# First attention layer: four modulation chunks computed as rows on TensorE, and the value product begun with the first four K-tiles

## What is computed

```python
c_act = jax.nn.silu(c)
mod = (c_act @ ada_w[layer] + ada_b[layer])[:, None, :]
sh_a, sc_a, gt_a, sh_m, sc_m, gt_m = jnp.split(mod, 6, axis=-1)
h = modulate(rms_norm(x, attn_norm[layer]), sh_a, sc_a)
mix = diff_attention(h, ...)      # (softmax(Q1 K1^T) - lambda softmax(Q2 K2^T)) V, 8 heads, RMSNorm, w_out
x = x + gt_a * mix
h = modulate(rms_norm(x, mlp_norm[layer]), sh_m, sc_m)
x = x + gt_m * squared_relu_mlp(h, mlp_w1[layer], mlp_w2[layer])
```

## Time and profile before

| | us |
|---|---|
| median of 3 runs | 1425.49 (1423.74 to 1425.61) |
| the profiled execution | 1421.12 |
| its span, first to last instruction | 1419.3 |
| granted TensorE clock, mean of the span | 0.968 of full |
| opening and first attention, up to the output projection | 156.0 |

### The profile page before, as it was taken

The page is one execution under the profiler, slowest core; times in us unless marked ns, Lnnn a source line. Parts: engine busy times, 40 slices in busy tenths (PEclk is TensorE's granted clock), DMA queues, the critical chain, the costliest instruction groups (busy, mean ns, idle before and its releaser), DMA issues. The chain is left out here.

```text
span 1419.3 us, 22085 instructions
## 1 busy us (share of the span) xinstructions
PE 1314.1 (93%) x8506; PEld 1136.6 (80%) x8506; DVE 876.9 (62%) x1546; ACT 678.7 (48%) x1184; POOL 170.4 (12%) x172
## 2 busy tenths in 40 slices
PE   6797989999989999899999878999999999899999
PEld 2687889888869865688998775699898777799987
DVE  2768678888675377696445674465555655555443
ACT  2354544334444356354544575464444565554442
POOL 0636101101000000010100121010000101011000
PEclk9889999999989899999999998999999999999999
DMA  9967639899866533259665251378655454376660
GB/s 351 317 211 248 199 104 331 291 326 321 288 194 175 172 117 93 81 159 301 178 194 158 87 184 34 103 193 261 188 171 185 135 178 133 92 206 184 188 178 30
DMA packets 249224, 267.42 MB, mean 188 GB/s; under 512 B 11040, under 2 KB 185376, under 8 KB 248736
## 3 DMA queue, kind: packets, MB, share of 16 engines
q1 hardware_dynamic: 246496, 263.52, 59.7%
q10 hardware_dynamic: 2624, 2.49, 0.5%
HBM read 264.83 MB, written 1.15 MB: 187 GB/s over the span
## 5 line engine op out<-in xcount | busy, mean ns | idle before, releaser
L1545 DVE TENSOR_TENSOR wlo<-wring,whi 128x1024 fp32r<-128x1024 f32 (+1 forms) x376 | 456.9, 1232 | 240.1 <-ACT whi L2607 239.4
L2607 ACT ACTIVATE whi<-wring 128x1024 fp32r<-128x1024 f32 (+1 forms) x376 | 388.8, 1043 | 360.4 <-PE ps_p L549 122.6
L547 PE MATMUL bank<-h_hi,whi 128*128 128x256 f32 x1216 | 351.5, 289 | 5.7 <-DVE h_lo L1699 2.3
L548 PE MATMUL bank<-h_lo,whi 128*128 128x256 f32 x1216 | 347.5, 286 | 0.0
L549 PE MATMUL bank<-h_hi,wlo 128*128 128x256 f32 x1216 | 347.1, 285 | 0.0
L547 PEld LDWEIGHTS bank<-h_hi,whi 128*128 128x128 f32 x1216 | 236.9, 195 | 11.8 <-issue 7.9
L548 PEld LDWEIGHTS bank<-h_lo,whi 128*128 128x128 f32 x1216 | 237.1, 195 | 0.7
L549 PEld LDWEIGHTS bank<-h_hi,wlo 128*128 128x128 f32 x1216 | 236.7, 195 | 0.0
L3244 POOL TENSOR_TENSOR ex<-ex 128x512 f32<-128x512 f32 x64 | 73.0, 1140 | 710.9 <-ACT g_hi L2716 710.9
L1767 DVE TENSOR_TENSOR g_lo<-ex,g_hi 128x512 fp32r<-128x512 f32 x64 | 45.0, 703 | 125.2 <-POOL ex L3244 125.0
L547 PE MATMUL bank<-whi,h_hi 128*128 128x512 f32 (+3 forms) x248 | 99.6, 402 | 14.4 <-DVE h_lo L1666 6.2
(11 more groups left out here) (375 smaller groups left out, 1878.8 us busy)
## 6 DMA issues: line engine op xcount, KB each, us to landing
wring<-in_mlp_w SPq DMA_DIRECT2D x128, 512.0 KB, 5.3
wring<-in_ada_w SPq DMA_DIRECT2D x96, 512.0 KB, 7.2
wring<-in_mlp_w_in SPq DMA_DIRECT2D x64, 512.0 KB, 4.8
wring<-in_mlp_w_out SPq DMA_DIRECT2D x64, 512.0 KB, 4.1
wring<-in_a_w_in SPq DMA_DIRECT2D x24, 512.0 KB, 5.7
wring<-in_moba_w_qkv SPq DMA_DIRECT2D x24, 512.0 KB, 4.4
wring<-in_kv_ada_w SPq DMA_DIRECT2D x16, 512.0 KB, 7.3
wring<-in_w_kv SPq DMA_DIRECT2D x12, 512.0 KB, 4.9
```

The costliest lines, as they stand in the source:

```text
L547: nc.tensor.matmul(out, lh, rh, start=first, stop=False)
L548: nc.tensor.matmul(out, lh, rl, start=False, stop=False)
L1545: v.tensor_tensor(piece_view(wlo, p), raw_view(p), piece_view(whi, p).bitcast(F32), ALU.subtract).then_inc(lo_ready, 1)
L2607: a.activation(piece_view(whi, p), raw_view(p), ACT.Copy).then_inc(hi_ready, 1)
```

## The change

1. No chunk is computed on POOL. DVE keeps chunks 4 (beside the value product) and 5 (in slot 4). Chunks 8, 9, 6 and 7 are computed as rows on PE, one each at the end of slots 0, 2, 5 and 7 (`ROW_SLOTS`, `ROW_CHUNKS`). Their columns are made at the end of the slot after (1, 3, 6, 8). ACT copies the row sums at the end of the row slot (into `xn`, which POOL used), DVE adds the bias two slots after it.
2. `weight_plan` puts all four loads of such a chunk behind the two loads of the head of that slot, where before the loads of two chunks were interleaved one each per head.
3. PE starts the value product's first two pieces (K-tiles 0 to 3) when the even halves are split, and waits for the odd halves ahead of the third piece. DVE writes `wlo` of piece t ahead of `split_odd` of tile t; ACT makes `whi` of piece 0 ahead of its first odd half. DVE goes up to two pieces further ahead during chunk 4.
4. `gate_rows("a0")` in slot 7 moves ahead of `diff_mix`. `late_rows` and `late_columns` of the second layer get numbers four higher. The number of loads and their bytes stay.

```diff
-MOD_SLOTS = (1, 4, 5)
+MOD_SLOTS = (1, 5)
+ROW_SLOTS = (0, 2, 5, 7)
+ROW_CHUNKS = (8, 9, 6, 7)
...
-             ada_part(4, 4), ada_part(8, 0), ada_part(4, 6)]
+             ada_part(4, 4), ada_part(4, 6)]
     for h in range(4):
-        plan += a_qk(h) + [ada_part(6, 2 * h), ada_part(*((8, 2 + 2 * h) if h < 3 else (9, 0)))]
+        plan += a_qk(h) + (ada(0, [ROW_CHUNKS[h // 2]]) if h % 2 == 0 else [])
     for j in range(4):
         plan += [a_v_part(1, j), ada_part(5, 2 * j)]
     for h in range(4, 8):
-        plan += a_qk(h) + [ada_part(7, 2 * h - 8)]
-        if h < 7:
-            plan += [ada_part(9, 2 * h - 6)]
+        plan += a_qk(h) + (ada(0, [ROW_CHUNKS[h // 2]]) if h % 2 == 0 else [])
...
-            turned("a0", TT - 1)
...
             for j in range(4):
+                if j % 2 == 0:
+                    pe.wait_ge(sem("a0_split"), TT + j)
                 token_piece(("a_v", 0), banks, h, j == 3)
...
+                if s == 7:
+                    gate_rows("a0", 16)
...
-                if s == 7:
-                    gate_rows("a0", 16)
-
-            pe.wait_ge(matvec_done, 4)
-            pool_columns([acc[:, 0, :]] + early[1], "early_mod", 2)
+                if s in ROW_SLOTS:
+                    late_rows(ROW_SLOTS.index(s))
+                if s - 1 in ROW_SLOTS:
+                    late_columns(ROW_SLOTS.index(s - 1))
+
...
             for t in range(TT):
+                keep_ahead("dve", t, 1)
                 split_odd("a0", t, outs)
-                keep_ahead("dve", t, 1)
...
             for j in range(4):
+                keep_ahead("dve", j, 3)
                 matvec(matvec_order[0], 2 * j, 2 * j + 2)
-                keep_ahead("dve", j)
...
-                    matvec(matvec_order[1 if head < 4 else 3], 2 * (head % 4), 2 * (head % 4) + 2)
                     keep_ahead("dve", p + 1)
...
+                if s - 2 in ROW_SLOTS:
+                    late_drain(ROW_SLOTS.index(s - 2))
...
-            pool_drain("early_mod", 7, 3, "ada_b0", 28)
+            late_drain(3)
...
+            keep_ahead("act", 0, 1)
             act.wait_ge(mod_drained, 4)
...
+                if s in ROW_SLOTS:
+                    late_sums(ROW_SLOTS.index(s))
```

More of the change, by code:

```diff
@@ L292, in build @@
                 "k": gate_row[:, :].rearrange("p (t c) -> p t c", t=TT)}
-        row_sums = [ex[:, :, :].rearrange("p a c -> p (a c)")[:, i * W:(i + 1) * W] for i in range(2)]
+        row_sums = [xn[:, i // 2, (i % 2) * W:(i % 2 + 1) * W] for i in range(4)]
+        row_sums += [ex[:, :, :].rearrange("p a c -> p (a c)")[:, i * W:(i + 1) * W] for i in range(2)]
         row_sums += [xn[:, 1, i * W:(i + 1) * W] for i in range(2)]
@@ L431, in build @@
         opening = (2, 3, 0, 1)
-        matvec_order = [ada_order[c] for c in (4, 6, 5, 7)] + ada_order[10:22] + ada_order[26:28]
-        drain_order = [ada_order[c] for c in opening + (4, 6, 5, 7, 8, 9)] + ada_order[10:]
+        matvec_order = [ada_order[c] for c in (4, 5)] + ada_order[10:22] + ada_order[26:28]
+        drain_order = [ada_order[c] for c in opening + (4, 8, 9, 5, 6, 7)] + ada_order[10:]
         def drained_by(*chunks):
             return max(drain_order.index(ada_order[c]) for c in chunks) + 1
-        early = (ada_order[8:10], [xn[:, 0, i * W:(i + 1) * W] for i in range(2)], xn[:, 1, 0:W])
-        late = ada_order[22:26]
+        late = [ada_order[c] for c in ROW_CHUNKS] + ada_order[22:26]
         ROOT_EIGHTH = math.sqrt(0.125)
@@ L463, in mod_columns @@
                                             start=True, stop=True)
[L464 to L473, removed]
                 last.then_inc(filled[b], 1)
@@ L1581, in mod_drain @@
                 v.memset(stat[:, 1:2], 0.0).then_inc(mod_drained, 1)
[L1583 to L1589, removed]
             def rstd(width, n, tag=None, eps=None):
@@ L2003, in diff_low, with late_drain @@
                                        ALU.mult, ALU.subtract).then_inc(sem("diff_low"), 1)
+            def late_drain(i):
+                key = ("late_mod", i)
+                layer, c = late[i]
+                src = bank_full(dve, key)
+                first, at = ada_index(late[i]), col["ada_b" + layer[3:]] + 4 * c
+                v.tensor_tensor(mod[:, 4 * first:4 * first + 4], src[:, 0:4], params[:, at:at + 4],
+                                ALU.add).then_inc(drained[uses[key][0]], 1)
+                bank_emptied(dve, key)
+                v.memset(stat[:, 1:2], 0.0).then_inc(mod_drained, 1)
             for j in range(4):
+                keep_ahead("dve", j, 3)
                 matvec(matvec_order[0], 2 * j, 2 * j + 2)
-                keep_ahead("dve", j)
             dve.wait_ge(sem("bias_in"), 16)
@@ L2774, in diff_high, with late_sums @@
                     sem("diff_high"), 1)
+            def late_sums(i):
+                key = ("late_rows", i)
+                a.activation(row_sums[i], bank_full(act, key), ACT.Copy).then_inc(drained[uses[key][0]], 1)
             for t in range(TT):
@@ L2812, in _ @@
             mlp("m0")
-            def late_sums(i):
-                key = ("late_rows", i)
-                a.activation(row_sums[i], bank_full(act, key), ACT.Copy).then_inc(drained[uses[key][0]], 1)
             norm("kv", [(h_hi, h_lo, gs, mod[:, 64:72]), (hk_hi, hk_lo, gs2, mod[:, 48:56])], 4, ready=(6, 8),
-                 last=last_of(("m0_w2", 7)), beside=late_sums)
+                 last=last_of(("m0_w2", 7)), beside=lambda t: late_sums(4 + t))
             def nsa_kv(w):
```

64 lines of the change are left out of this document (13 added, 51 removed).

## The result

The changed kernel takes 1439.16 us (1438.03 to 1441.93, four runs), the kernel before 1425.55 beside it: ratio 1.0097, 95% interval 1.0074 to 1.012, so 10.5 to 17.1 us slower. The forecast was 1432.9 with a range of 1424.0 to 1438.5: the direction was right, the size too small by 6.3 us, and the range ends 0.7 us too low.

A forecast was written before the change was run, and what follows sets the result against it. Bound by DMA rate until about 57 us, then by who gives back places in the ring of ten loads. Terms 0.85 + 1.75 + 4.45 + 0.4 - 1.85 + 1.8 = +7.4 us on 1425.49 gave 1432.9, range 1424 to 1438.5.

The forecast's parts named there:

- R(2): Eight row matmuls of chunk 6 on PE at the end of slot 5, booked at +1.75 us.
- low clock: PE's clock falls in slot 6's new wait and the work behind it runs slower: +1.8 us, bounds 0 and 3.1.
- Opening: Until about 57 us: value product ends 5.4 us early, all lost to later waits for transfers; booked at nothing.
- Rival 1: The early start survives and slot 6's two terms go: 1421.6 us, chance 0.17; decided if chunk 8's row matmuls end before 54.
- Price of a chunk: On PE's path, a chunk's row matmuls take 1.75 us (bounds 1.05 and 3.8), its columns one slot later 0.82.
- Slot 5: Head 5's first piece lands 2.3 us later, silent GpSimd gives 1.5 back; head 3's weights come at 121.75: +0.85 us.
- Slot 6: Main term: head 7's loads wait for R(2), so PE waits 3.8 us ahead of diff_back(3): +4.45 us.
- Slot 7: Its earlier 1.3 us of waiting goes and chunk 7's row matmuls come at its end: +0.4 us.
- GpSimd: Silent in slot 5, so DVE's next step and wlo return to their usual 1.53 and 1.22 us: 1.5 us back.
- Rival 3: Every block of row matmuls holds the stream; slot 6's stall returns in slots 1 and 3: +12, 1437.9 us, chance 0.13.
- Rival 2: Trade, no change: head 7's loads arrive just in time and the clock holds: +1.2, 1426.7 us, chance 0.14.
- sign of 2 us: Behind about 164 us the length stays as before; the forecast is wrong if it differs by over 2 us.

The follow-up runs named there:

- e3: Kernel before with only the early value product and its order of splits; chunks 8 and 9 stay on GpSimd: 1424.91 us, ratio 0.9998.
- e6: e2 with diff_combine of head 3 moved in DVE's slot 4 behind the second pair of chunk 5's steps: 1427.62 us.
- e12: e2 with loads of chunks 8, 9 behind heads 1, 3, their row matmuls ending slots 1, 2, and every late_drain right behind diff_even; second measurement: 1420.08 us.
- e1: Changed kernel with the drain of chunk 9's columns moved to the head of chunk 5's steps in DVE's slot 4: 1436.02 us.
- e9: Changed kernel with chunk 9's drain first, as in e1, and only chunk 6's four loads moved behind head 5's: 1424.82 us.
- e2: Changed kernel with chunk 9's drain first, as in e1, and loads of chunks 6 and 7 behind those of heads 5 and 7: 1422.17 us.
- e11_changed_again: Changed kernel as it is, measured again in five rounds beside the kernel before: 1439.84 us, ratio 1.0107.

## Why the prediction was wrong in size

By its own steps, forecast against the windows above and the earlier trace rows, in us; slot 5 is what the forecast's own dates give (110.0 to 130.05 against 16.9):

| step | forecast | measured |
|---|---|---|
| up to the start of slot 4 | +0.45 | +1.7 |
| slot 4 | -1.0 | -0.7 |
| slot 5 with R(2) | +3.15 | +8.6 |
| slot 6 with M | +4.45 | +5.6 |
| slot 7 with R(3) | +0.4 | +3.9 |
| slot 8 with M | -1.85 | -1.7 |
| low clock | +1.8 | in the slots |
| sum | +7.4 | +17.4 |

**Opening: right in what it books, in part by luck.** R(0) ends at 57.6 (57.4 forecast), head 1 starts at 60.55 (60.4), head 0's weights come at 78.95 (78.3). Nothing of the early start survives, and e3 shows it alone. But the value product starts at 36.2 (34.9 forecast) and ends at 49.5 (46.6): its first 5.1 us run at a granted clock of 0.52. And R(0) does not wait for its loads, as the forecast had it; PE reaches it late, at 55.7, and runs it in one go:

```profile
55.70 1.92 PE L701 MATMUL bank<-wring,pos_f 128*32 128x512 f32 x16
```

That its end is the forecast one is chance. That the transfers set the pace shows one step later, where head 1's product waits 2.9 us for `wlo` and ACT before it 6.7 us for the load. Rival 1 is out.

**Price of a chunk: right at the high clock.** R(2) takes 1.9 us (135.16 to 137.02; 1.75 forecast), M at the end of slot 3 0.9 (97.18 to 98.11; 0.82). At the low clock, in e6, a block takes 3.6 us, near the bound of 3.8. With four row blocks on PE e12 is faster than before.

**Slot 5: the step that failed,** "Weights at 121.75: +0.85". The turns came 9.3 us later than before, for two reasons. The first is a size: head 5's first piece came 5.2 us later (its `wlo` starts on DVE at 119.52, before at 114.29), not 2.3. I let the held loads of the block run in a row behind one release at 107, at 1.35 us each. The queue's timeline, then two windows of 1 us behind it:

```profile
108.08 2.01 SPq L3237 DMA_DIRECT2D wring<-in_ada_w  x3
```

```profile
113.00:114.00 1.00, 0.00 (x0) 0.00 (x0) 0.00 (x0) 0.00 (x0) 0.00 (x0) 1.00 0.80 262
...
115.00:116.00 1.00, 0.00 (x0) 0.00 (x0) 0.00 (x0) 0.00 (x0) 0.00 (x0) 1.00 1.13 353
```

The first of chunk 6's held loads goes out at 108.1, 1.1 us after the forecast's date, and from there to ACT's start on the piece it takes 10.3 us and not 8.4. The third load goes out 1.6 us behind the first (a later step of DVE releases it), and a load takes 1.5 to 2.0 us at 353 to 262 GB/s; which of the two makes the 1.9 us is not shown. Less the 1.5 us that the silent GpSimd gives, the piece makes the weights 3.7 us late (124.52). The second reason is a mechanism that the sum lacked and put at nothing: the product ahead of the wait takes a bank that the drain of chunk 9's columns gives back, and this drain stands on DVE behind the very work that PE would have waited for anyway. The kernel has PE wait for a drained bank whenever it takes one (`bank_take`); I had not asked where the drain stands in DVE's own queue. The wait and the product are then not side by side but in a row: 5.6 us more to the turns. e1 gives 5.3 of them back at the turns and 2.9 at the end of the slot, the rest goes to the low clock.

**Slot 6: right, and the main term for the forecast.** 3.8 us of wait forecast, 3.5 measured, for the reason given. e9 sharpens it: not the hold but the two loads ahead of head 7's piece made it long. M behind the wait runs at the low clock (148.10 to 149.66, 1.6 us for the 0.82 of the forecast).

**Slot 7: half missed.** Behind slot 6's wait the clock is low: the first product of slot 7 takes 4.8 us (149.66 to 154.45), its second 3.0 (155.73 to 158.69). The difference is the +1.8 of the sum. With `diff_back` and M of slot 6 at the low clock too (2.0 us for the forecast's 1.0) the low clock cost 2.8 us, inside its bounds of 0 and 3.1 but more than booked. A second wait for a drain (L895, 1.2 us) was not in it. With both, slot 7 comes to +3.4 of the +3.9. In e12, with the drains at the head, that wait is gone.

**GpSimd: right.** Its work in these slots is down to a few short steps for the heads' norms. Durations of `wlo` on DVE, min, median and max in ns from 30 to 200, against the earlier trace rows:

```profile
L1540 DVE TENSOR_TENSOR wlo<-wring,whi x34: 1214/1225/1227, 34.5 to 196.6; 128x1024 fp32r<-128x1024 f32 x34
```

It now never takes over 1.23 us in this stage; before, its longest was 2.32. The Trainium skill ("SBUF — State Buffer", section "SBUF: two separate sides") says that these two engines share ports; by it the longest `wlo` should fall to the usual one when GpSimd is silent, and it did: from 2.32 to 1.23 us. The gain was eaten: DVE was waiting for loads.

**The rivals.** Rival 3, that every R holds the stream, was priced at +12 and put into slots 1 and 3. The sum is nearer to its number than to mine, but not through its mechanism. R(1) does hold the stream, for 17.6 of SyncE's 50.9 us for L701 (in slot 2), and no stall of PE follows in slot 3 (9.27 busy of 9.31). R(2) holds it for 12.5, which is the wait of slot 6, and R(3) for 20.7, where only loads of `a_out` wait. Ahead of slot 5's stall it is not a row block that holds the queue but DVE's steps; SyncE's waits from 92 to 112:

```profile
SPq L3237 <- DVE acc L1559: 12.4, 2, 11.7
```

Rival 2 (head 7's loads just in time, the clock holds) is out by slot 6's wait.

**What stays open.** The stage is 17.4 us longer in both profiles of the changed kernel, the medians differ by 13.6 and 14.9. The interval of the first ends below it (17.1 us). The interval of the second measurement (12.8 to 17.7 us) holds 17.4; whether executions without a profile lose 2 us less in this stage can't be told from these runs.

## What to carry over

In this kernel, where a ring of places is fed in order, the place of a load counted for more than its bytes, which stayed the same: before moving work to an engine that uses four loads at once, look for the piece that the in-order engines take next, and put the block behind it. And when a step is handed to another engine, follow its result to the instruction that gives back its buffer, and ask what that one stands behind; here the drain did best at the head of a slot, where its input was long ready.

## What the runs showed of the hardware

Not expected: how long the clock stays low is not in proportion to the wait before it. In the kernel before, PE works for 3.8 us at a granted clock of 0.53 behind a wait of 7.25; in the changed kernel for 5.1 us at 0.53 behind 13.6, and for 6.3 us at 0.51 behind 3.5; in e6 for 9.1 us at 0.50 behind 5.8. What work falls into the stretch then sets the price: from the start of the row matmuls of chunk 6 to the scores of slot 6, the same instructions, it is 7.6 us in e6 (126.14 to 133.72) and 4.9 in e2 (124.48 to 129.39). Why one stretch is longer than another these runs don't show.

The stretch behind the output projection, the same instructions in every kernel here, takes 1264.5 us in one profile of the changed kernel and 1270.5 in the next (windows of e11_changed_again, the columns as above):

```profile
35.20:173.41 138.21, 110.65 (x728) 94.75 (x729) 67.08 (x160) 60.91 (x140) 5.61 (x10) 0.87 0.68 217
173.41:1443.90 1270.49, 1200.68 (x7732) 1046.57 (x7731) 779.22 (x1345) 611.85 (x1035) 107.30 (x123) 0.97 0.58 177
```

PE's busy time is 5 us longer there with the same count of records. A difference of two profiled spans is uncertain by as much, and the prediction's sign of 2 us for this stretch asked for more than a profile can tell; the stage ahead of it, read from the two traces, repeats to 0.1 us.
